# Seam between the mLSTM chunks and attention: less work in the last chunk, two quotients on VectorE, the first attention steps issued earlier

## What is computed

```python
def step(carry, inp):
    c_mat, n_vec, m_prev = carry
    ...
    num = (einsum('bhts,bhse->bhte', s, vb) + inter_w[..., None] * einsum('bhtd,bhde->bhte', qb, c_mat))
    den = sum(s, axis=-1) + inter_w * einsum('bhtd,bhd->bht', qb, n_vec)
    h = num / maximum(abs(den), exp(-m_t))[..., None]
    ...
    c_new = decay[..., None, None] * c_mat + einsum('bhsd,bhse->bhde', kb * w_s[..., None], vb)
    n_new = decay[..., None] * n_vec + einsum('bhs,bhsd->bhd', w_s, kb)
    return (c_new, n_new, m_new), h
...
h = h * rsqrt(mean(h * h) + eps)          # per head, then norm weight and sigmoid gate
...
p = softmax(where(valid, q @ k_selected * scale, -inf)); att = p @ v_selected
```

## Time and profile before

| | |
|---|---|
| median of three runs | 2338.13 us |
| the profiled execution: its own time | 2340.59 us |
| the profiled execution: its span | 2338.8 us |
| TensorE busy, share of the span | 93% |
| VectorE, ScalarE, GpSimd busy | 79%, 58%, 24% |
| granted TensorE clock, mean of the span | 0.951 |
| TensorE's share of the chain that ended last | 69% |

### The profile page before, as it was taken

One profiled execution on the slowest core, in us unless ns is written; L12 is line 12 of the kernel. 1 busy time (PEld: TensorE's weight loads), 2 busy tenths in 40 slices (PEclk: granted clock), 3 DMA queues, 4 the chain that ended last, 5 costly groups with the idle time before them and its releaser, 6 DMA issues.

```text
span 2338.8 us, 41558 instructions
## 1 busy us (share of the span) xinstructions
PE 2166.9 (93%) x15487; PEld 1731.9 (74%) x15487; DVE 1836.9 (79%) x2152; ACT 1365.3 (58%) x1545; POOL 560.8 (24%) x434
## 2 busy tenths in 40 slices
PE   6899999868899399999999999999999999999994
PEld 5677888645778377778778778778778778778773
DVE  3699999948733767877877877877877877877886
ACT  4542223875742457667667667667667667667665
POOL 1007786665000112112112112112112112112120
PEclk9769999967999699999999999999999999999997
DMA  5011211021023379889889889889889889889897
GB/s 142 19 46 37 55 46 49 29 66 44 1 93 118 105 261 341 311 287 349 309 284 349 310 285 349 313 285 351 309 286 347 313 285 347 311 285 347 315 370 260
DMA packets 253598, 526.46 MB, mean 225 GB/s; under 512 B 33048, under 2 KB 59800, under 8 KB 253180
## 3 DMA queue, kind: packets, MB, share of 16 engines
q1 hardware_dynamic: 240268, 483.27, 57.6%
q0 software_dynamic: 13264, 42.34, 7.5%
HBM read 490.96 MB, written 35.91 MB: 225 GB/s over the span
## 4 chain that ended last, share of the span: by engine, by line
PE 69%; DMA 10%; DVE 9%; ACT 5%; issue 4%; POOL 2%; SPq 0%; DVEq 0%; ACTq 0%; POOLq 0%
PE ps L1763 13%; PE ps L1765 12%; PE ps L1764 12%; DMA e_raw<-in_w_gate_up_dram 9%; PE ps L1770 9%; PE ps L1431 5%; PE ps L1432 5%; PE ps L1433 5%; DVE e_wlo L2262 2%; PE ps L1775 1%; PE ps L1506 1%; PE ps L1651 1%; PE ps L1640 1%; ACT a_p L1235 1%; DVE a_s L2040 1%
## 5 line engine op out<-in xcount | busy, mean ns | idle before, releaser
L1314 ACT ACTIVATE e_whi<-e_raw 128x2048 fp32r<-128x2048 f32 x411 | 785.8, 1917 | 421.5 <-PE ps L1765 313.4
L2262 DVE TENSOR_TENSOR e_wlo<-e_raw,e_whi 128x2048 fp32r<-128x2048 f32 x410 | 926.5, 2284 | 66.9 <-ACT e_whi L1314 65.3
L1763 PE MATMUL ps<-e_whi,xh 128*128 128x512 f32 x1088 | 434.7, 400 | 0.0
L1764 PE MATMUL ps<-e_whi,xl 128*128 128x512 f32 x1088 | 424.3, 390 | 0.0
L1765 PE MATMUL ps<-e_wlo,xh 128*128 128x512 f32 x1088 | 424.1, 390 | 0.0
L942 POOL DMA_INDIRECT x_d<-ym,scur x34 | 73.0, 2146 | 861.9 <-ACT ym L1347 841.5
L1763 PEld LDWEIGHTS ps<-e_whi,xh 128*128 128x128 f32 x1088 | 204.3, 188 | 52.7 <-issue 12.7
L1765 PEld LDWEIGHTS ps<-e_wlo,xh 128*128 128x128 f32 x1088 | 204.2, 188 | 44.0
L1763 PE MATMUL ps<-e_whi,ath 128*128 128x512 f32 x544 | 221.6, 407 | 13.1 <-DVE atl L2290 13.1
L1764 PEld LDWEIGHTS ps<-e_whi,xl 128*128 128x128 f32 x1088 | 204.5, 188 | 39.3
L1765 PE MATMUL ps<-e_wlo,ath 128*128 128x512 f32 x544 | 213.2, 392 | 0.0
(11 more groups left out here) (351 smaller groups left out, 3348.8 us busy)
## 6 DMA issues: line engine op xcount, KB each, us to landing
e_raw<-in_w_gate_up_dram SPq DMA_DIRECT2D x275, 1024.0 KB, 6.7
e_raw<-in_w_down_dram SPq DMA_DIRECT2D x136, 1024.0 KB, 11.4
w_raw<-in_w_in_dram SPq DMA_DIRECT2D x20, 512.0 KB, 3.8
xt<-in_x_dram SPq DMA_DIRECT2D x8, 512.0 KB, 6.2
xr<-in_x_dram SPq DMA_DIRECT2D x8, 512.0 KB, 4.3
x_d<-x SPq DMA_DIRECT2D x8, 512.0 KB, 2.6
h_d<-h SPq DMA_DIRECT2D x8, 512.0 KB, 2.9
x<-x_d SPq DMA_DIRECT2D x8, 512.0 KB, 7.2
```

The costliest lines, as they stand in the source:

```text
L1314: nc.scalar.activation(e_whi[:, m % HRING, :], e_raw[:, m % RING, :], ACT.Copy).then_inc(s.e_hi, 1)
L1763: nc.tensor.matmul(dst, a_hi, slot_hi, start=False, stop=False, skip_group_check=True)
L1764: nc.tensor.matmul(dst, a_lo, slot_hi, start=False, stop=False, skip_group_check=True)
L2262: nc.vector.tensor_tensor(e_wlo[:, m % HRING, :], e_raw[:, m % RING, :], e_whi[:, m % HRING, :].bitcast(F32), ALU.subtract).then_inc(s.e_l ...
```

## The change

- In the last chunk (c = 7) the state is no longer brought forward: its keys are not transposed or scaled, up(7), its copy, the state decay and the state add are gone.
- quotient(6) and quotient(7) run on VectorE, as a maximum of 4 columns, a reciprocal and the product; VectorE issues quotient(6) ahead of `k_lo` and quotient(7) behind `q_lo` and ahead of the masks. GpSimd does six quotients instead of eight.
- `k_hi` and `q_hi` of block 0 move on ScalarE from the start of pass 8 into pass 7, behind weights(7).
- scores(0) move on TensorE from pass 9 into pass 8, ahead of transpose(6); exp(0) and exp(1) move on ScalarE ahead of m_mt(7). The wait for all mixes now stands ahead of the first `a_t`; TensorE's wait for m_mt(7) stands ahead of scores(4) instead of scores(2).
- SP's wait for the last up is lowered by one, since there is one fewer.

```diff
@@ -227,6 +227,7 @@
         self.v_score = sem("v_score")
         self.v_topk = sem("v_topk")
         self.v_mask = sem("v_mask")
+        self.v_last = sem("v_last")
         self.p_mcol = sem("p_mcol")
         self.v_mcol = sem("v_mcol")
         self.a_mexp = sem("a_mexp")
@@ -670,7 +671,7 @@
 
 
             sp.wait_ge(s.g_mix, NT)
-            sp.wait_ge(s.p_up, NT)
+            sp.wait_ge(s.p_up, NT - 1)
             for c in range(KC):
                 if c < 4:
                     for k in range(KVH):
@@ -831,7 +832,7 @@
 
             def m_weights(c):
 
-                gp.wait_ge(s.a_s1, 2 * c + 2)
+                gp.wait_ge(s.a_s1, 2 * c + 2 if c + 1 < NT else 2 * NT - 1)
                 if c >= 1:
                     gp.wait_ge(s.p_nd, c)
                 nc.gpsimd.tensor_tensor(m_w[:], m_sc[:], m_ex[:], ALU.mult).then_inc(s.g_w, 1)
@@ -875,7 +876,7 @@
             for c in range(NT + 2):
                 if c < NT:
                     m_weights(c)
-                if 1 <= c <= NT:
+                if 1 <= c <= NT - 2:
                     m_quotient(c - 1)
                 if c >= 2:
                     m_mix(c - 2)
@@ -883,6 +884,7 @@
                     m_root(c - 1)
                 if c < NT:
                     m_sum(c)
+                if c + 1 < NT:
                     m_state(c)
 
 
@@ -1142,7 +1144,7 @@
 
             def m_weights(c):
 
-                act.wait_ge(s.p_s1, 2 * c + 2)
+                act.wait_ge(s.p_s1, 2 * c + 2 if c + 1 < NT else 2 * NT - 1)
                 if c >= 1:
                     act.wait_ge(s.g_w, c)
                 for h in range(MH):
@@ -1155,6 +1157,17 @@
                     m = nc.scalar.activation(dst[:, 2 * k:2 * k + 2, :], ps[:, bank + k, 0:2 * (MD + 1)].rearrange("p (h n) -> p h n", h=2), ACT.Copy)
                 m.then_inc(signal, 1)
 
+            def exp(u):
+                i, h = u // HEADS, head(u)
+                w = P * (i + 1)
+                act.wait_ge(s.v_nm, u + 1)
+                if u >= 2:
+                    act.wait_ge(s.p_pt, u - 1)
+                if u >= 2 * HEADS:
+                    act.wait_ge(s.v_rs, u - 2 * HEADS + 1)
+                nc.scalar.activation(a_p[:, u % 2, 0:w], a_s[:, u % 2, 0:w], ACT.Exp, scale=HD ** -0.5, bias=nmx[:, u % 2:u % 2 + 1],
+                                     accum_out=rs[:, (i % 2) * 8 + h:(i % 2) * 8 + h + 1]).then_inc(s.a_exp, 1)
+
             def q_hi_of(i):
                 if i >= 2:
                     act.wait_ge(s.p_s, HEADS * (i - 1))
@@ -1162,19 +1175,23 @@
 
             m_keys(0)
             for c in range(NT + 2):
-                if c == NT:
+                if c < NT:
+                    m_weights(c)
+                if c + 1 < NT:
+                    act.wait_ge(s.p_up, c + 1)
+                    act.wait_ge(s.g_st, c + 1)
+                    m_out(m_up, 3, s.a_up)
+                if c + 2 < NT:
+                    m_keys(c + 1)
+                if c == NT - 1:
                     act.wait_ge(s.g_rq, 15)
                     act.wait_ge(st_mo[0], 32)
                     act.wait_ge(st_mo[1], 32)
                     nc.scalar.activation(k_hi[:], kt[:], ACT.Copy).then_inc(s.a_qkhi, 1)
                     q_hi_of(0)
-                if c < NT:
-                    m_weights(c)
-                    act.wait_ge(s.p_up, c + 1)
-                    act.wait_ge(s.g_st, c + 1)
-                    m_out(m_up, 3, s.a_up)
-                if c + 1 < NT:
-                    m_keys(c + 1)
+                if c == NT + 1:
+                    exp(0)
+                    exp(1)
                 if c >= 2:
                     act.wait_ge(s.p_m3, c - 1)
                     if c >= 3:
@@ -1224,17 +1242,6 @@
                     act.wait_ge(s.a_at, t + 1)
                 nc.scalar.activation(mx_hi[:, t % 2, :, :], mixt[:, :, t * P:(t + 1) * P], ACT.Copy).then_inc(s.a_mxhi, 1)
 
-            def exp(u):
-                i, h = u // HEADS, head(u)
-                w = P * (i + 1)
-                act.wait_ge(s.v_nm, u + 1)
-                if u >= 2:
-                    act.wait_ge(s.p_pt, u - 1)
-                if u >= 2 * HEADS:
-                    act.wait_ge(s.v_rs, u - 2 * HEADS + 1)
-                nc.scalar.activation(a_p[:, u % 2, 0:w], a_s[:, u % 2, 0:w], ACT.Exp, scale=HD ** -0.5, bias=nmx[:, u % 2:u % 2 + 1],
-                                     accum_out=rs[:, (i % 2) * 8 + h:(i % 2) * 8 + h + 1]).then_inc(s.a_exp, 1)
-
             def pt_out(u):
                 i = u // HEADS
                 act.wait_ge(s.p_pt, u + 1)
@@ -1245,8 +1252,6 @@
                                      ACT.Copy).then_inc(s.a_pt, 1)
 
             act.wait_ge(s.g_mix, NT)
-            exp(0)
-            exp(1)
             for u in range(NT * HEADS):
                 pt_out(u)
                 if u + 2 < NT * HEADS:
@@ -1592,16 +1597,16 @@
             m_weights(0)
             for c in range(NT + 2):
                 mt = slice(4 + c * P, 4 + (c + 1) * P)
-                if c < NT:
+                if c < NT and c >= 1:
+                    pe.wait_ge(s.a_nd, c)
+                if c + 1 < NT:
                     pe.wait_ge(s.a_s1, 2 * c + 1)
-                    if c >= 1:
-                        pe.wait_ge(s.a_nd, c)
                     for h in range(MH):
                         m = nc.tensor.matmul(pair_of_heads(h, 3), m_kw[:, c % 2, h, :], mvtok[:, c, h, :], start=True, stop=True)
                     m.then_inc(s.p_up, 1)
-                if c + 1 < NT:
+                if c + 2 < NT:
                     m_keys(c + 1)
-                if c == NT + 1:
+                if c == NT:
                     pe.wait_ge(s.a_nd, NT)
                     scores(0)
                 if c >= 2:
@@ -1613,7 +1618,8 @@
                     m.then_inc(s.p_m3, 1)
                 if c < NT:
                     pe.wait_ge(s.g_w, c + 1)
-                    pe.wait_ge(s.a_up, c + 1)
+                    if c + 1 < NT:
+                        pe.wait_ge(s.a_up, c + 1)
                     for h in range(MH):
                         m = nc.tensor.matmul(pair_of_heads(h, 3), m_w[:, h, :], mvtok[:, c, h, :], start=True, stop=True)
                     m.then_inc(s.p_nd, 1)
@@ -1652,8 +1658,9 @@
                                              start=(b == 0), stop=(b == i), skip_group_check=True)
                 m.then_inc(s.p_pv, 1)
 
-            pe.wait_ge(s.a_mt, NT)
             for u in range(0, NT * HEADS, 2):
+                if u == 2:
+                    pe.wait_ge(s.a_mt, NT)
                 if u + 2 < NT * HEADS:
                     scores(u + 2)
                 transposes(u)
@@ -2013,6 +2020,20 @@
                 w = P * (u // HEADS + 1)
                 nc.vector.tensor_scalar(a_p[:, u % 2, 0:w], a_p[:, u % 2, 0:w], r, None, ALU.mult).then_inc(s.v_arow, 1)
 
+            last = Steps(dve, s.v_last)
+
+            def quotient(c):
+
+                dve.wait_ge(s.a_abs, c + 1)
+                dve.wait_ge(s.g_h, NT - 2)
+                last(nc.vector.tensor_tensor(mden, mabs, mexp[:, c, 2, 0:MH], ALU.max))
+                last.done()
+                last(nc.vector.reciprocal(mrd, mden))
+                last.done()
+                dve.wait_ge(s.a_hn, c)
+                nc.vector.tensor_tensor(m_h[:], m_n[:, :, 0:MD], mrd.unsqueeze(2).to_broadcast([P, MH, MD]), ALU.mult).then_inc(s.g_h, 1)
+
+            quotient(NT - 2)
             dve.wait_ge(s.a_qkhi, 1)
             nc.vector.tensor_tensor(k_lo[:], kt[:], k_hi[:].bitcast(F32), ALU.subtract).then_inc(s.v_qklo, 1)
 
@@ -2022,6 +2043,7 @@
                                         q_hi[:, i % 2, :, :].bitcast(F32), ALU.subtract).then_inc(s.v_qklo, 1)
 
             q_lo_of(0)
+            quotient(NT - 1)
 
             def mx_lo_of(t):
                 dve.wait_ge(s.a_mxhi, t + 1)
```

## The result

| | before | after |
|---|---|---|
| median | 2338.88 us (6 runs, 2337.08 to 2340.97) | 2325.39 us (6 runs, 2323.9 to 2330.1) |
| profiled execution: its own time, its span | 2340.59, 2338.8 us | 2326.24, 2324.4 us |
| granted TensorE clock, mean | 0.951 | 0.955 |

The ratio of the two is 0.9945 with a 95% interval of 0.9935 to 0.9956: 13.5 us off, where 5.8 were forecast and 10 was the most that the range allowed. The direction was right, the size was not.

A forecast was written before the change was run, and what follows sets the result against it. The bound was taken as one serial GpSimd and ScalarE path from chunk 7's `m_w` to attention's first exponential, in a hole of TensorE. 4.2 + 1.6 = 5.8 us off 2338.13 gave 2332.3 us, range 2328.0 to 2336.6.

The forecast's parts named there:

- the seam: Stretch between the last mLSTM chunk and attention: 4.2 us off up to square(7) plus 1.6 from the exponentials, 5.8 in all.
- quotient(6): On VectorE it takes 1.1 us; square(6), standing behind `m_nd`, starts 0.5 us earlier.
- Abs(7): On ScalarE, without state decay and state add, it starts at 498.75 instead of 499.92: 1.2 us earlier, quotient(6)'s 0.5 included.
- quotient(7): On VectorE it takes 1.15 us where GpSimd took 5.2: 4.05 us less.
- Given back behind m_mt(6): Square(7) must wait on ScalarE for m_mt(6) and starts at about 501.15, so 1.0 us of quotient(7)'s gain is lost.
- exps moved out: At attention's start, mix(7) releases the first `a_t` directly, without exp(0), division and transposition between: 1.6 us more.
- state work: In the last chunk, no state decay or state add: abs(7) 1.2 us earlier, 0.5 of it from quotient(6).
- GpSimd's weight splits and SP's loads depend on mix(7) and come 4.2 earlier, with the same length: In attention, the output-weight splits and their loads start 4.2 us earlier and keep their length.
- the sign: Stated test: the prediction is wrong if attention's end moves by another amount than the first `a_t`.
- More than the sum: Rival, 0.13: block 2's `q_lo` may escape the splits (1.7 us), faster seam clock 1 to 2.5 more; gain 7 to 10.
- The first rival: Chance 0.23: VectorE and GpSimd stop each other at the new places; gain only 3.4 to 5, 2333.5 to 2334.8 us.
- Slower, through the clock: Rival, 0.04: less TensorE work in pass 7 and shifted scores leave TensorE longer at 1.2 GHz; 2343 us or more.

The follow-up runs named there:

- paced kernels: Kernel before and changed kernel, each with GpSimd's weight splits cut into 24 pieces released by VectorE's divisions: 2326.19 us and 2318.73 us.
- a_place: Changed kernel with five of eight output-weight chunks loaded earlier and splits started at the 14th reciprocal of attention, nearly the old place: 2328.7 us.
- a_early13: Changed kernel with five of eight output-weight chunks loaded earlier and splits waiting for the 13th division, 1.2 us earlier than in a_place: 2332.6 us.
- b_gate15: Kernel before with one wait added, so GpSimd starts the weight splits only after VectorE has divided unit 14: 2330.59 us, ratio 0.9961.
- p_quot: Kernel before with splits in 24 paced pieces and, of the change, only both quotients on VectorE, ahead of `k_lo`: 2322.57 us, ratio 0.9937.

## Why the prediction was wrong, and where it was right

**Right: the seam.** Forecast 4.2 + 1.6 = 5.8, measured 6.28 in the pair of paced kernels and 6.57 between the two profiles, each from `m_w` of chunk 7 on.

- *quotient(6)*: forecast 1.1 us, measured 0.39 + 0.18 + 0.69. It gained nothing beyond `m_nd`, as said: square(6) waits behind it.
- *Abs(7)*, forecast at 498.75: 498.56, though `m_w` started 0.54 later (491.34) in this run (489.1 to 490.9 in the four other kernels with this seam). TensorE's product of `m_w` and values took 1.38 us there instead of 2.1, at a granted clock of 0.79 instead of 0.50. In a_place's profile it took 2.10 again, at 0.50, and transpose(6) 0.67 instead of 1.13, at 1.00. So the clock gives 0.5 or 0.7 us somewhere in the seam; it is what the sum lacks.
- *quotient(7)*, forecast 1.15: 498.80 to 499.91, 1.1 us. *Given back behind m_mt(6)*: square(7) at 500.82, right behind it, as forecast (501.15).
- *exps moved out*: the first `a_t` follows mix(7) at once. Forecast 1.6; from mix(7)'s start to the first `a_t` 1.30 us against 2.88.
- By parts, the order had been state work 1.2 (0.5 of it quotient(6)), quotient(7) 4.05 less 1.0, exponentials 1.6; alone they measured 1.56 for the state work without quotient(6), 2.88 for both quotients and 1.64.

**Wrong: the step "GpSimd's weight splits and SP's loads depend on mix(7) and come 4.2 earlier, with the same length".** The length was right. The start came 3.3 earlier and not 4.2: mix(7) started 4.35 earlier, but from there to the first split 19.2 us passed instead of 18.1, and no run says why the loads took longer. What failed is that the step priced the splits at nothing, and so took it that their cost to VectorE stays. The sum lacked a term: what the splits cost attention, before and after. It measured 14.1 us before and 7.7 after by the pairs with spread splits, 6.4 less. Between the two profiles, q_lo(1) to q_lo(4) is 5.95 us shorter (53.33 and 47.38 us). The forecast missed 13.5 - 5.8 = 7.7 us; about 6 of it are this term, 0.5 to 0.8 the seam's, and the rest is the part behind the routing, where the runs spread.

The prediction had named the sign: it would be wrong if "the end of attention moved by another amount than the first `a_t` did". The first `a_t` moved by 5.9 us, q_lo(4) by 12.0. That the splits came to a cheaper place was luck and no part of the design: with the same seam and the splits started 3.8 us earlier in attention (a_early13) half of the gain is gone.

The rows for it had been read. `q_lo` at 2.39 us against 0.69 was priced as one stall in a rival, 1.7 us for "More than the sum", where nine divisions and the next `q_lo` met the splits too. That rival had the mechanism and a size nearly four times too small (1.7 against 6.4); its other term, a faster clock at the seam for 1 to 2.5 us, gave 0.5 to 0.7. The first rival had the same mechanism with the sign turned: the splits, later in attention's work by 1.6 us, were to cost about 1 more on wider divisions. They came later by 2.8 us (13.37 against 10.61 behind q_lo(1)), block 3 did cost 2.2 more, but block 2 7.3 and block 1 0.8 less. (The times given for that rival are off by up to 0.5 us: gains of 5.1 to 3.4 from 2338.13 are 2333.0 to 2334.7.)

The Trainium skill (SBUF — State Buffer, section "Who interferes with whom") says that a VectorE `tensor_scalar` too can run in a mode that takes the ports which VectorE shares with GpSimd, and that the second comer is then fully blocked. By that rule a division, which is a `tensor_scalar`, can wait for a whole split of 2.35 us, and the rows agree: 2.07 and 2.54 us above. I had read it for instructions with two inputs only and applied it to the new places of three of them, and not to the 29 us in which both engines run all the time.

**Rival "Slower, through the clock"**: the clock rose earlier, not later: in block 2 it was granted 0.78 instead of 0.50. It rose where the splits moved, with the old seam too (b_gate15), and is worth little of the gain: 0.5 us in block 2 for 0.10 of clock between the paced kernels, about 2 us at most over blocks 1 to 3 by the estimate under the table.

## What to carry to other kernels

- Where a change shifts two engines against each other, price the whole stretch in which both run, not the moved instructions: sum, over each shape, its duration there less its shortest elsewhere. Here that sum was 13.8 us before the change, more than twice what the edit itself gives.
- Such a cost jumps with the place (a stretch of 8 to 14 us for shifts of 0.2 to 7 us), so it is better taken out than aimed at: short pieces, each released by the semaphore of the other engine's last conflicting instruction. That took 13.6 us off the kernel before (2339.83 to 2326.19, measured together), as much as the whole change under study.
- Judge a part by the distance between two instructions of the trace. The medians of these kernels can't part 2 us; the seam's length, the same to 0.3 us in five kernels with the changed seam, could part 1.3.

## What the hardware showed that I had not expected

- A VectorE division with one input in SBUF (`a_p` times a column) waits out a GpSimd cast or subtraction as a subtraction with two inputs does: it ends 0.14 to 0.30 us behind it, `q_lo` 0.55. `k_lo`, begun 0.38 us before the end of `m_w`, took 1.45 us instead of 1.23.
- It holds the other way too: beside `k_lo` and `q_lo` four maxima of one column on GpSimd took 2.6 instead of 1.08, and a power 1.86 instead of 1.03.
- An instruction on four columns waits as well. Four columns' maximum on VectorE took 0.39 us for quotient(6) and 0.16 for quotient(7) in the changed kernel, and 0.39 both times in p_quot. Each time that it took 0.38 or 0.39 GpSimd's state add ran beside it, and it ended 0.02 or 0.03 us behind the add; where the state add is gone it took 0.16 or 0.17. The changed kernel and p_quot:

```profile
488.67 1.27 POOL L868 TENSOR_TENSOR state<-state,m_up 128x516 f32<-128x516 f32 x1
...
497.36 1.28 POOL L868 TENSOR_TENSOR state<-state,m_up 128x516 f32<-128x516 f32 x1
...
498.27 0.39 DVE L2028 TENSOR_TENSOR cols<-cols 128x4 f32<-128x4 f32 x1 [8.97 <-ACT cols L1223]
```

- Two profiles of nearly the same seam differ by 0.7 us in one product, by the clock that was granted during it (0.79 and 0.50).
